# The last 171 decode-attention steps moved into the linear-attention stage, on four of the eight banks

## The reference, cut to what matters

```python
def diff_attn_sample(q, k, v, cache_k, cache_v, layer, page_table, lam, rel_bias):
    kp = cache_k[layer, page_table].reshape(B, past, DIFF_HEADS, 2, DIFF_DK)
    vp = cache_v[layer, page_table].reshape(B, past, DIFF_HEADS, DIFF_DV)
    a = softmax(concat([q . kp * DIFF_SCALE + bias, q . k * DIFF_SCALE + bias]))
    p = a[:, :, 0] - lam * a[:, :, 1]
    return p[..., :past] @ vp + p[..., past:] @ v

def gla_chunk(S, q, k, v, lg):                  # a chunk of 128 tokens; S is 64 x 128 for each head
    b = cumsum(lg)
    o = (q * exp(b)) @ S + (causal sum over s of (q_t exp(b_t - b_s) k_s)) @ v
    S_new = exp(b_last) * S + (k * exp(b_last - b)).T @ v
    return S_new, o

def merge_out(h, o_d, dg, o_g, gg, ...):
    og = rms_norm(o_g, gla_norm_w) * silu(gg)   # GLA's norm, per head
    return h + concat([od, og]) @ w_out
```

## Time and profile before

| | us |
|---|---|
| median of two runs | 1194.19 (1192.83 and 1195.55) |
| the profiled execution | 1189.06 |
| its span, first to last instruction | 1187.4 |
| projection with decode steps | to 763.7 |
| linear attention | 763.7 to 893.7 |
| prompt attention and output | 893.7 to 1187.4 |

### The profile page before, as it was taken

The page is one execution under the profiler, slowest core; times in us unless marked ns, Lnnn a source line. Parts: engine busy times, 40 slices in busy tenths (PEclk is TensorE's granted clock), DMA queues, the critical chain, the costliest instruction groups (busy, mean ns, idle before and its releaser), DMA issues. The chain is left out here.

```text
span 1187.4 us, 26574 instructions
## 1 busy us (share of the span) xinstructions
PE 1042.8 (88%) x9099; PEld 843.7 (71%) x9099; DVE 571.8 (48%) x1434; ACT 464.0 (39%) x1327; POOL 259.7 (22%) x416
## 2 busy tenths in 40 slices
PE   4999999999999999888899999556685899989988
PEld 3899999967677775666676776345564688778755
DVE  4755533434352331342434342379866766666422
ACT  5633312433442322332333443235424654554321
POOL 0000100012222221221222234399401111111200
PEclk9999999999999999999999999868885799999989
DMA  6423645479897865775898887561104122211101
GB/s 187 126 86 95 202 143 181 143 247 322 306 316 244 280 222 163 257 227 180 280 306 297 284 262 239 155 236 53 54 9 120 36 94 83 71 37 56 53 23 43
DMA packets 109433, 199.44 MB, mean 168 GB/s; under 512 B 15050, under 2 KB 49300, under 8 KB 109300
## 3 DMA queue, kind: packets, MB, share of 16 engines
q1 hardware_dynamic: 73892, 117.23, 31.8%
q0 software_dynamic: 20480, 67.13, 16.5%
q10 hardware_dynamic: 14928, 13.38, 3.4%
HBM read 178.87 MB, written 19.60 MB: 167 GB/s over the span
## 5 line engine op out<-in xcount | busy, mean ns | idle before, releaser
L259 POOL DMA_DIRECT2D vraw<-in_cache_v x256 | 138.0, 539 | 615.6 <-issue 611.3
L1061 PE MATMUL bank<-wh,xTh 128*128 128x256 f32 (+1 forms) x864 | 252.2, 292 | 11.9 <-DVE qwr L1269 9.8
L1061 PE MATMUL bank<-wh,xTl 128*128 128x256 f32 (+1 forms) x864 | 244.9, 283 | 0.0
L1061 PE MATMUL bank<-wl,xTh 128*128 128x256 f32 (+1 forms) x864 | 244.7, 283 | 0.0
L477 DVE COPY kt<-bank 128x512 f32<-128x512 f32 x128 | 88.6, 692 | 182.8 <-PE bank L280 118.8
L1061 PEld LDWEIGHTS bank<-wh,xTh 128*128 128x128 f32 (+1 forms) x864 | 161.7, 187 | 20.3 <-DVE qwr L1269 11.6
L1061 PEld LDWEIGHTS bank<-wh,xTl 128*128 128x128 f32 (+1 forms) x864 | 161.3, 187 | 0.0
L1061 PEld LDWEIGHTS bank<-wl,xTh 128*128 128x128 f32 (+1 forms) x864 | 161.1, 186 | 0.0
L280 PE MATMUL bank<-ident,kraw 128*128 128x128 f32 x1024 | 153.3, 279 | 0.4 <-DVE kt L477 0.3
L401 ACT ACTIVATE kt<-bank 128x512 f32<-128x512 f32 x128 | 76.2, 595 | 158.8 <-PE bank L280 158.2
L280 PEld LDWEIGHTS bank<-ident,kraw 128*128 128x128 f32 x1024 | 112.8, 141 | 22.5 <-issue 21.6
(11 more groups left out here) (241 smaller groups left out, 1827.8 us busy)
## 6 DMA issues: line engine op xcount, KB each, us to landing
vraw<-in_cache_v POOLq DMA_DIRECT2D x256, 256.0 KB, 4.6
kraw<-in_cache_k SPq DMA_DIRECT2D x256, 256.0 KB, 4.0
wraw<-in_w_in SPq DMA_DIRECT2D x28, 512.0 KB, 4.9
out<-nat ACTq DMA_DIRECT2D x32, 128.0 KB, 2.2
wo_raw<-in_w_out SPq DMA_DIRECT2D x8, 512.0 KB, 9.3
xr<-in_x_prompt SPq DMA_DIRECT2D x7, 512.0 KB, 3.6
out<-xr SPq DMA_DIRECT2D x7, 512.0 KB, 2.6
bT<-in_x_prompt SPq DMA_DIRECT2D x4, 512.0 KB, 4.6
```

The costliest lines, as they stand in the source:

```text
L259: pool.dma_start(vraw[:, p % VR, :], cache_v.rearrange("a n p h d -> (a n) p (h d)")[bass.ds(page, 1)] .rearrange("o p c -> (o p) c")).the ...
L1061: ins = pe.matmul(z_at(u)[0:r, 0:CB], a[:, k, P * i:P * i + r], b[:, wslot(c), k, :], start=(n == 0), stop=(n == 3 * KT - 1))
```

## The change

Of the 665 decode steps the projection now does 494, spread over the same uses; the other 171 are done in the linear attention: 27 ahead of its tile loop and three at each of six places in each of the first eight tiles. Since the steps hold banks 4 to 7, the linear attention keeps to banks 0 to 3: its products use two banks in two groups, one after the other, and key turns, state products and turned mixtures share one. The states get blocks of zeros (64 x 128 next to each head's own), so that one matmul of 128 x 256 serves two heads and the zero-padded queries `qz` go. ACT takes the squares from PSUM and copies the output scaled by the root; POOL multiplies it with the gate. Value pages are loaded on SP from step 494 on, together with the keys; values and gates of the tiles on ACT; the output weights only after the last decode step. The diff, cut:

```diff
-        PAUSE = NSUB
+        G_FIRST, G_EACH = 27, 3
+        PAUSE = NSUB - G_FIRST - G_EACH * 6 * (TILES - 1)
...
+        values_by = [nc.gpsimd]
...
-        def decode_pool(pool):
+        def decode_values():
             def load_value(p):
+                eng = values_by[0]
                 if p >= VR:
                     b, g = (p - VR) // NPAGES, (p - VR) % NPAGES // GRP
-                    pool.wait_ge(pv_done, b * RG + g + 2)
+                    eng.wait_ge(pv_done, b * RG + g + 2)
...
-            sp_ = g2.take("state_p", [P, 2, DV])
-            ss_ = g2.take("state_s", [P, NB, 2, DV])
+            sp_ = g2.take("state_p", [P, 2, 2 * DV])
+            ss_ = g2.take("state_s", [P, NB, 2, 2 * DV])
...
-            pA = bank[:, 0:4, :]
-            pOg, pK, pdS, pM = bank[:, 4, :], bank[:, 5, :], bank[:, 6, :], bank[:, 7, :]
+            pA, pOg, pX = bank[:, 0:2, :], bank[:, 2, :], bank[:, 3, :]
...
+            def decoded(i, place):
+                return min(PAUSE + G_FIRST + G_EACH * (6 * i + place + 1), NSUB)
...
             def _(sp):
...
+                values_by[0] = sp
+                for x in range(PAUSE + 1, NSUB + 1):
+                    go_values(x)
+                    go_sp(x)
+                sp.wait_ge(od_added, NB)
                 for k in range(KT):
                     sp.dma_start(wo_raw[:, k, :], w_out[0, k * P:(k + 1) * P, :]).then_inc(wo_in, 16)
...
-                for m in range(2):
-                    sp.dma_start(s_sample[0].rearrange(...)[m], ss_[:, :, m, :]).then_inc(g_out, 16)
-                    sp.dma_start(s_prompt[0, 0].rearrange(...)[m], sp_[:, m, :]).then_inc(g_out, 16)
+                for h in range(H):
+                    half, c = slice(DK * (h % 2), DK * (h % 2) + DK), slice(h % 2 * DV, (h % 2 + 1) * DV)
+                    sp.dma_start(s_sample[0, :, h].rearrange("b d e -> d b e"), ss_[half, :, h // 2, c]).then_inc(g_out, 16)
+                    sp.dma_start(s_prompt[0, 0, h], sp_[half, h // 2, c]).then_inc(g_out, 16)
...
             def _(pe):
+                def turn_k(i):
+                    if i >= 2:
+                        pe.wait_ge(mgo, i - 1)
...
+                        ins = pe.transpose(pX[0:r, m * P:(m + 1) * P], ff[:, i % 3, LV, 1, m, 0:r], ident[:])
...
+                go_pe(PAUSE + G_FIRST)
+                products(0, 0)
+                products(0, 1)
+                turn_k(0)
                 for i in range(TILES):
                     if i + 1 < TILES:
-                        products(i + 1)
+                        products(i + 1, 0)
+                        go_pe(decoded(i, 0))
+                        if i + 1 < TILES - 1:
+                            products(i + 1, 1)
+                        go_pe(decoded(i, 1))
                     output(i)
-                    state(i)
+                    if i + 1 < TILES:
+                        go_pe(decoded(i, 2))
                     if i >= 1:
                         turn_mix(i - 1)
-                turn_mix(TILES - 1)
+                    if i + 1 < TILES:
+                        go_pe(decoded(i, 3))
+                        turn_k(i + 1)
+                        go_pe(decoded(i, 4))
+                    state(i)
+                    if i + 1 < TILES:
+                        go_pe(decoded(i, 5))
...
             def _(act):
                 def out(i):
                     act.wait_ge(ogd, i + 1)
+                    for h in range(H):
+                        ins = act.activation(squares_g[0:r, c], pOg[0:r, c], ACT.Square, accum_out=r4g[0:r, 0, h:h + 1])
+                    linked(ins)
+                    linked(act.activation(r4g[0:r, 1, :], r4g[0:r, 0, :], ACT.Ln, scale=1.0 / DV, bias=eps_g[0:r, :]))
+                    linked(act.activation(r4g[0:r, 2, :], r4g[0:r, 1, :], ACT.Exp, scale=-0.5))
                     if i >= 1:
                         act.wait_ge(mgd, i)
-                    act.activation(og[0:r, :], pOg[0:r, :], ACT.Copy).then_inc(ogc, 1)
...
+                        ins = act.activation(og[0:r, c], pOg[0:r, c], ACT.Copy, scale=r4g[0:r, 2, h:h + 1])
+                    ins.then_inc(ogc, 1)
...
+                go_act(PAUSE + G_FIRST // 3)
                 decays(0)
+                load_v(0); load_v(1)                 # after the stores of the projection
+                go_act(PAUSE + 2 * G_FIRST // 3)
                 decays(1)
+                go_act(PAUSE + G_FIRST)
                 turned_k(0)
                 for i in range(TILES):
                     if i + 2 < TILES:
                         decays(i + 2)                # with go_act(decoded(i, 0)) inside
+                    go_act(decoded(i, 1))
                     out(i)
+                    go_act(decoded(i, 2))
                     if i >= 1:
                         mixed(i - 1)
+                    go_act(decoded(i, 3))
+                    turned_k(i + 1)
+                    go_act(decoded(i, 5))
+                    if i >= 1 and i + 1 < TILES:
+                        act.wait_ge(ogd, i); act.wait_ge(dsd, i); act.wait_ge(mgd, i)
+                        load_v(i + 1)
...
             def _(pool):
+                def norm(i):
+                    pool.wait_ge(ggd, i + 1)
+                    pool.wait_ge(ogc, i + 1)
+                    if i >= 1:
+                        pool.wait_ge(mgt, i)
+                    pool.tensor_tensor(mixg[0:r, :], og[0:r, :], gg[0:r, i % 2, :], ALU.mult).then_inc(mgd, 1)
+                for hh in range(2):                  # zeros beside each head's own block
+                    pool.memset(sp_[off[0], :, off[1]], 0.0).then_inc(off_zero, 1)
+                    pool.memset(ss_[off[0], :, :, off[1]], 0.0).then_inc(off_zero, 1)
                 exponents(pool, linked, 1)
+                exponents(pool, linked, 2)
                 for i in range(TILES):
-                    if i + 2 < TILES:
-                        exponents(pool, linked, i + 2)
+                    if i + 3 < TILES:
+                        exponents(pool, linked, i + 3)
                     gate(i)
+                    norm(i)
...
             def _(dve):
-                factors(0)
-                factors(1)
+                go_dve(PAUSE + G_FIRST // 3)
+                factors(0, 0); factors(0, 1)
+                go_dve(PAUSE + 2 * G_FIRST // 3)
+                factors(1, 0); factors(1, 1)
+                go_dve(PAUSE + G_FIRST)
+                masks(0, 0); masks(0, 1)
                 for i in range(TILES):
-                    masks(i)
                     if i >= 1:
                         state(i - 1)
-                        norm(i - 1)
-                    if i + 2 < TILES:
-                        factors(i + 2)
+                    if i + 1 < TILES:
+                        go_dve(decoded(i, 0))
+                        masks(i + 1, 0)
+                        go_dve(decoded(i, 1))
+                        if i + 1 < TILES - 1:
+                            masks(i + 1, 1)
+                        go_dve(decoded(i, 2))
+                        if i + 2 < TILES:
+                            factors(i + 2, 0)
+                        go_dve(decoded(i, 3))
+                        if i + 2 < TILES:
+                            factors(i + 2, 1)
+                        go_dve(decoded(i, 5))
                 state(TILES - 1)
-                norm(TILES - 1)
...
                 load_qk(1)                           # SP, prompt attention
+                sp.wait_ge(g_out, 128)
                 load_v(0)
```

More of the change, by code:

```diff
@@ L186, in hymba_kernel @@
         v_in = [sem(f"v_in{n}") for n in range(VR)]
+        v_late = [sem(f"v_late{n}") for n in range(2)]
         c_in = sem("c_in")
@@ L1442, in products @@
                         if i >= 1:
-                            pe.wait_ge(amask, groups_done(i - 1, g))
-                        for n in group:
-                            s1, t0 = (HALVES[0], HALVES[0]) if n == 0 else (r, 0)
-                            for h in range(H):
-                                half = slice(DK * (h % 2), DK * (h % 2) + DK)
-                                c0 = (n % 2) * 256 + (h // 2) * P
-                                ins = pe.matmul(pA[0:s1, 2 * (n // 2) + h % 2, c0 + t0:c0 + r],
-                                                ff[half, i % 3, n, 1, h // 2, 0:s1],
-                                                ff[half, i % 3, n, 0, h // 2, t0:r], start=True, stop=True)
@@ L1453, in products @@
-                        ins.then_inc(adone, 1)
-                    if i >= 1:
-                        pe.wait_ge(kdo, i)
+                            pe.wait_ge(amask, groups_done(i - 1, 1))
+                    else:
+                        pe.wait_ge(amask, groups_done(i, 0))
+                    for n in level_groups(i)[g]:
+                        s1, t0 = (HALVES[0], HALVES[0]) if n == 0 else (r, 0)
+                        for h in range(H):
+                            half = slice(DK * (h % 2), DK * (h % 2) + DK)
```

(30 more changed lines are left out.)

226 lines of the change are left out of this document (109 added, 117 removed).

## The result

The changed kernel takes **1215.8 us** (median of two runs, 1215.3 to 1216.3) against 1194.2 before: a ratio of 1.018 with a 95% interval from 1.013 to 1.023, slower by its interval, where 1185 was forecast. The profiled execution took 1215.3 us, with a span of 1213.5 against 1187.4.

What follows compares the result with a forecast made beforehand. TensorE bounds the projection and last stage, VectorE, in order, the linear attention. The projection loses 67 us, the linear attention gains 57.5 (34 + 58.5 + 56 + 10 + 29 = 187.5 against 130.0): −9.5, forecast 1185 us, range 1149 to 1216.

Steps and rivals of the forecast that it cites:

- the lower clock: Rival, linear attention: TensorE at 1.2 GHz throughout, five tiles and the tail's output slower, 30 us more, 1215 us; chance 0.07.
- What leaves the projection: Projection: 171 decode steps move out and 67 us go, with bounds of 60 and 75 us.
- The steps inside: Linear attention: 0.53 us per heavy step in start and heavy tiles; light tiles pay a third of 18 × 0.26 us.
- The four banks: Linear attention: with four banks for eight, each tile becomes a chain through all engines; stage 187.5 us with steps, 130.0 before.
- A light tile, 14 us.: Linear attention, tiles 3 to 6: chain 11.5 us, hand-overs 1.1, steps 1.6; 14 us each, 56 for four.
- The start, 34 us,: Linear attention before and into the first tile: first decays 5.5 us, 27 steps 14.3, two blocks 12, products and masks 5.
- The tail, 29 us,: Linear attention from tile 7's state update on: 29 us as before, norm overlap saving 3, eight stores adding 2.9.
- the heavy tiles: Linear attention, tiles 0 to 2 with heavy decode steps: 19.5 us each, 58.5 us for three.
- the eighth tile: Linear attention, tile 7: one group and no factors behind it, 10 us.
- One queue for all pages: Rival: value loads on SP wait with key loads, so TensorE waits for pages; 50 us added, 1235 us; chance 0.10.
- The stage fills up: Rival, linear attention: steps fill every gap, VectorE's 120 us plus 30 set the stage at 150; 1147 us; chance 0.28.
- the 11.6 that I had as the most: Linear attention: nine norms on POOL could cost VectorE up to 11.6 us through shared ports; left out of the sum.

Runs made afterwards that it cites:

- experiment 1: The changed kernel with none of the 171 decode steps inside the linear attention, all 665 in the projection: 1246.1 us, ratio 1.047 to the kernel before.
- 11: The changed kernel with no steps inside, turns first, tile loads earlier, exponents' memsets first, stores split, sample states loaded later, POOL issuing all values: 1208.4 us.
- experiment 5: The changed kernel without steps inside, plus spare identity turns on TensorE in the tiles and tail, into a bank nothing reads: 1235.2 us, ratio 1.036.
- experiment 12: The changed kernel, 171 steps inside, plus 8 spare identity turns on TensorE at two places per tile from the fourth tile on, none in the tail: 1204.3 us.
- experiment 4: The changed kernel with the turns of mixture and keys, and their copies, ahead of each tile's output on TensorE and norm on ScalarE: 1196.2 us, ratio 1.004.
- experiment 3: The changed kernel with POOL's new memsets of the states behind its memsets of the exponents instead of ahead: 1210.9 us, ratio 1.016.
- experiment 6: The changed kernel with the last four value pages that POOL issues in the projection issued by SP, first in the linear attention: 1214.9 us, ratio 1.019.
- Experiment 7: The changed kernel, 171 steps inside, with turns first, tile loads earlier, exponents' memsets first, last four value pages on SP, state stores on two queues: 1188.3 us.

## Why the prediction was wrong

The 1215.8 us lie just inside the stated range, whose upper end, 1216, was set for the lower clock. That is luck: the forecast was a gain, the kernel lost, and most of the loss has other causes than that rival's.

**What leaves the projection** was right: 72 us for 67, within the bounds of 60 to 75.

**The steps inside** were about right in sum: with steps left out, my terms give 34 - 14.3 for the start, 3 x 12.4 for the heavy tiles without theirs, 4 x 12.4 for the light ones, 10 and 29, some 145 us, so 42 for the steps; experiments 1 and 11 show 46 and 47 behind the two orders by the traces (43 and 45 by the medians and the microseconds that left the projection).

**The four banks** are the term that failed. I had 145 us for the stage without steps, 16 more than before; experiment 1 measured 184.1, 52 more than before. These 36 to 39 us are the whole of the miss (26.1 us of span lost where 9.5 were to be won); the steps, 4 us dearer, and the projection, 5 us better, cancel. Of the 39, the start and first tile of experiment 1 have 11 (42.9 for 32.1), the next seven tiles 15 (99.6 for 84.4) and the tail 13 (41.6 for 29). Three steps of the sum hid them.

*A light tile, 14 us.* The chain was listed rightly, ScalarE's norm in it, and at a granted clock of 0.91 it took 12.6. But I worked it out with TensorE at full speed and treated the lower clock as a rival of 0.07 and an upper bound. In these tiles it comes with the chain: from 800 to 808 us TensorE was busy for 3.0 of 8 us, the granted clock went from 1.00 to 0.50, and TensorE's own links of the chain grew (the second group of products takes 1.79 us at 856.87 and 1.09 at 842.35). The four tiles took 67.0 us for 56. Experiment 5 is the plainest test: with the order unchanged and the clock brought to 0.91, the seven tiles take 84.4 us, my price for them (the tenth is chance). With the steps inside, experiment 12 takes 11.5 us back with the order unchanged, and experiment 4 takes 20 with nothing added. The two overlap: with the turns first TensorE waits less, and the mean clock from the fourth to the eighth tile is 0.84 where it was 0.79. The rival's time, 1215, is where the changed kernel landed, but only in part by the rival's path. Of its 30 us, five light tiles were to take 22.5 more and took 13.7 (79.7 for 66), and the tail's output 8 more, while that output ran at the full clock (1.00 from 884 to 892 us). What the rival left out were the start, the tail's order and the order that brings the lower clock about in the tiles.

*The start, 34 us,* took 47.7. Two edits that I counted at nothing stand on its path: POOL's memsets (3.8 us, experiment 3), which I named under POOL's sum and not in its order, and the end of the projection, where POOL's last page load now comes as late as the last matmul and its drain holds all engines for 4.4 us (experiment 6). I did not ask who waits for POOL's last loads to finish. The start also holds 27 steps at 0.71 of the clock, for which I had the full-speed 0.53 us; that they make up the rest, some 5 us, is argued and not shown.

*The tail, 29 us,* took 39.3. Eight stores took 7.2 us from 913.31 on for 3.1, which is 4.1 more where I had 2.9, and the 3 us that the norm was to give back did not come. The nine updates begin 16.5 us after the tile before, for 12.7: the state products wait for a copy of the mixture that ScalarE makes behind the last norm (892.1 to 895.5 us). Most of them run 1.70 us apart for 1.43 of work and wait 0.28 for TensorE's state products, which ran at the lower level, 0.50, with TensorE busy for 15.8 of the 16 us from 896 on. So here the clock stayed low through 16 us of nearly steady work, as in experiment 5's tail, and no run says why. Experiment 7 brought the stretch from 39.7 to 30.2 us, with the turns first, the loads earlier and the stores split all at once; no run parts these.

*The rest:* the heavy tiles took 63.3 us for 58.5, at a clock of 0.87, and the eighth tile 12.7 for 10.

**The rivals.** *One queue for all pages* fell: no page wait is in TensorE's list. The rule of the Trainium skill on issuing engines (DMA: Bandwidth & Descriptors, "Issuing engines are not separate DMA queues"), that several of them save only the time to issue, agrees with this trace: SP alone issued the pages of this stage, with a median of 3.0 us from issue to landing. *The stage fills up* fell: VectorE was busy for 107 of 230 us.

The rule of the Trainium skill on the shared ports (SBUF — State Buffer, "SBUF: two separate sides"), agrees with the trace too, but with the cost on the other side than I had it. By it, of a VectorE instruction with two inputs from SBUF and a POOL instruction that reads SBUF, whichever starts first holds the ports to its end while the other blocks:

```profile
754.11 1.48 DVE L1754 TENSOR_TENSOR ff<-ff,gkT 128x1280 f32<-128x1280 f32 x1
...
754.94 1.79 POOL L1722 TENSOR_TENSOR mix_g<-og,gg 128x512 f32<-128x512 f32 x1 [17.48 <-ACT og L1613]
```

VectorE's product had begun first and took its usual 1.48 us; POOL's norm, 0.65 us of it beside that product, took 1.79 where a norm alone takes 1.26. At 814.93 us a norm lies 1.45 us beside such a product and takes 2.58. All five norms that met one began behind it. They cost POOL 2.7 us together, and VectorE 0.3, in a product at 796.60 that began beside a norm, not the 11.6 that I had as the most.

**What stays open:** how the 20 us of experiment 4 part between the order itself and the clock that it brings back. In the kernels without steps the mended order wins 23.4 us in seven tiles at 0.77, and spare matmuls win 15.2 in the old order at 0.91; both act on the same waits, and no run here holds the clock still while the order changes.

## What to carry to other kernels

When a stage gives up buffers, write its chain out in each engine's own order: a short copy that frees a shared bank belongs ahead of the long one, or everything behind that bank pays for both. Test what fills a stage and what the stage costs unfilled apart from each other, before adding the two: here the filling was worth its price, and the emptier stage was the loss. When a wait is removed at a stage's start, look which semaphore comes last next, and take off it whatever only a later part needs.

## What the runs showed that I had not expected

- Work added to TensorE made the kernel faster, twice: by 11 us without steps (clock in the tiles 0.69 to 0.91) and by 11.5 with them (0.69 to 0.84, then 1.00). In a stage where TensorE waits in every tile, the lower of the two clock levels (0.50) is part of the price of the waits. It is not a sure cure: in the tails of the changed kernel and of experiment 5 TensorE ran at 0.50 while busy nearly throughout.
- After a value page that POOL issued at 692.28 us, POOL began its next instruction at 701.46, and all engines with it. With the last four pages moved to SP they began at 697.10. In that run and in the kernel before POOL's drain was as much as 7.2 and 5.4 us long, but ended before the other engines' work and held nobody.
- Four state loads of 256 KB each, issued ahead of the pages, held VectorE for 11.2 us through a shared semaphore, in a stretch where the DMA engines were busy for about 0.7 of the time.
